# Peer routing stage: expert rows fetched a batch ahead, u's high part multiplied first, GELU stores on ScalarE's queue, and the second u tile's low part on VectorE

## The reference, cut to what matters

```
q = (xt @ w_q).reshape(T, PEER_HEADS, 2, PEER_HALF)
s = jnp.einsum('thpc,hpnc->thpn', q, sub_keys)
s_top, i_top = lax.top_k(s, PEER_TOPK)                     # 16 of 128 keys, twice per head
cand_s, cand_i = ...                                       # all 16 x 16 pairs
best_s, pos = lax.top_k(cand_s, PEER_TOPK)                 # 16 of 256 pairs, 8 heads
idx, gate = ..., jax.nn.softmax(best_s)                    # 128 experts of 16384 for each token
act = jax.nn.gelu(jnp.einsum('tkd,td->tk', u_tab[ib], xb), approximate=False)
out = jnp.einsum('tk,tkd->td', act * gb, v_tab[ib])
```

## Time and profile before

| what | value |
|---|---|
| median of 3 runs | 1585.91 us (1579.07 to 1590.8) |
| profiled execution | 1588.34 us, span 1586.6 us |
| PE busy | 1471.9 us (93%) |
| DVE busy | 1274.1 us (80%) |
| ACT busy | 824.7 us (52%) |
| POOL busy | 506.2 us (32%) |
| mean granted PE clock | 0.976 of 2.4 GHz |

### The profile page before, as it was taken

The page is one execution under the profiler, slowest core; times in us unless marked ns, Lnnn a source line. Parts: engine busy times, 40 slices in busy tenths (PEclk is TensorE's granted clock), DMA queues, the critical chain, the costliest instruction groups (busy, mean ns, idle before and its releaser), DMA issues.

```text
span 1586.6 us, 25321 instructions
## 1 busy us (share of the span) xinstructions
PE 1471.9 (93%) x9438; PEld 1325.3 (84%) x9438; DVE 1274.1 (80%) x2444; ACT 824.7 (52%) x1571; POOL 506.2 (32%) x425
## 2 busy tenths in 40 slices
PE   7999799999989888888897888999989999999999
PEld 6898688789889888888897887889878888888887
DVE  4638787776798697877867876999989999999997
ACT  4553453151434656655665854554455556565553
POOL 4011620110466666656661111322322222222220
PEclk9999899999999999989999999999999999999999
DMA  6220004030465788887889998999899999999993
GB/s 201 81 81 1 8 29 162 28 125 35 143 209 181 270 289 285 282 269 259 286 285 394 369 353 307 379 379 372 328 414 410 410 410 409 407 411 405 409 401 124
DMA packets 168439, 420.49 MB, mean 265 GB/s; under 512 B 12896, under 2 KB 100096, under 8 KB 151680
## 3 DMA queue, kind: packets, MB, share of 16 engines
q1 hardware_dynamic: 140608, 251.10, 44.8%
q0 software_dynamic: 27712, 167.82, 27.1%
HBM read 372.44 MB, written 46.40 MB: 264 GB/s over the span
## 4 chain that ended last, share of the span: by engine, by line
PE 55%; DMA 7%; DVE 4%; issue 4%; POOL 3%; ACT 2%; SPq 1%; ACTq 0%; DVEq 0%
PE bank L2432 7%; PE bank L2434 7%; PE bank L2433 7%; PE bank L2108 5%; PE bank L2109 5%; PE bank L2110 5%; DMA early_gelus<-early_gelu 5%; PE bank L2127 4%; PE banks L2432 3%; PE banks L2434 3%; PE banks L2433 3%; POOL u_split L2008 2%; PE bank L2420 2%; PE bank L2421 2%; PE bank L2422 2%
## 5 line engine op out<-in xcount | busy, mean ns | idle before, releaser
L2108 PE MATMUL bank<-x_hi,u_split 128*128 128x320 f32 x832 | 268.7, 323 | 7.8 <-POOL u_split L2008 7.3
L2109 PE MATMUL bank<-x_lo,u_split 128*128 128x320 f32 x832 | 260.3, 313 | 0.0
L2110 PE MATMUL bank<-x_hi,u_split 128*128 128x320 f32 x832 | 259.8, 312 | 0.0
L1804 POOL DMA_INDIRECT scores<-in_peer_uv,pair_index x86 | 106.7, 1241 | 392.2 <-DVE pair_sum L1828 391.2
L2108 PEld LDWEIGHTS bank<-x_hi,u_split 128*128 128x128 f32 x832 | 160.7, 193 | 12.2 <-issue 9.8
L2479 ACT ACTIVATE act_tile<-onehots 128x384 f32<-128x384 f32 x128 | 124.3, 971 | 82.3 <-DVE act_lo L2521 76.9
L2127 PE MATMUL bank<-onehot_j,onehot_gated 128*128 128x128 f32 x768 | 109.2, 293 | 58.6 <-issue 42.0
L2109 PEld LDWEIGHTS bank<-x_lo,u_split 128*128 128x128 f32 x832 | 160.4, 193 | 0.0
L2110 PEld LDWEIGHTS bank<-x_hi,u_split 128*128 128x128 f32 x832 | 159.8, 192 | 0.0
L2127 PEld LDWEIGHTS bank<-onehot_j,onehot_gated 128*128 128x128 f32 x768 | 100.9, 204 | 65.8 <-issue 65.1
L2008 POOL TENSOR_TENSOR u_split<-u_raw,u_split 128x1024 fp32r<-128x1024 f32 x41 | 99.2, 2420 | 119.8 <-ACT u_split L2165 61.2
(11 more groups left out here) (433 smaller groups left out, 4037.0 us busy)
## 6 DMA issues: line engine op xcount, KB each, us to landing
v_raw<-in_peer_v SPq DMA_DIRECT2D x128, 512.0 KB, 10.7
u_raw<-in_peer_u SPq DMA_DIRECT2D x64, 512.0 KB, 5.5
u_raw_more<-in_peer_u SPq DMA_DIRECT2D x64, 512.0 KB, 4.9
gates<-gate_stage SPq DMA_DIRECT2D x24, 1024.0 KB, 11.6
onehots<-gates SPq DMA_DIRECT2D x32, 768.0 KB, 11.6
early_gelus<-early_gelu SPq DMA_DIRECT2D x104, 160.0 KB, 4.8
gelu_tile<-early_gelus SPq DMA_DIRECT2D x104, 160.0 KB, 11.3
w_raw<-in_w_in SPq DMA_DIRECT2D x9, 1024.0 KB, 5.0
```

The costliest lines, as they stand in the source:

```text
L1804: pool.indirect_dma_start(self.slot(k), None, self.table, bass.IndirectOffsetOnAxis(ap=self.sidx[:, k:k + 1], axis=0)).then_inc(self.lande ...
L2108: nc.tensor.matmul(out, uh[:, q, w], m.xh[:, k, P + NS:], start=(k == 0), stop=False)
L2109: nc.tensor.matmul(out, uh[:, q, w], m.xl[:, k, P + NS:], start=False, stop=False)
L2110: t = nc.tensor.matmul(out, ul[:, q, w], m.xh[:, k, P + NS:], start=False, stop=(k == KD - 1))
```

## The change

Four edits, all in `routing`:

1. POOL fetches the rows one batch ahead: four fetches ahead of batch 0, then in each batch the two of the next batch, and they now stand ahead of the batch's low part.
2. POOL makes only the low part of a batch's first u tile. The second one's (24 tiles) goes to DVE, which makes the low parts of batch n+1 in its round n, right after `oj` of batch n and ahead of the selection part and the dots.
3. PE multiplies the 16 high-part matmuls of a u tile after a wait for `u_hi` alone, then waits for the low part, then multiplies the 8 low-part ones.
4. The GELU store goes from SP's list to ACT's, right behind the GELU. SP's list keeps the loads and the stores of gates.

```
-    pool_lows = list(range(1, FIRST)) + [t for n in range(LATE) for t in ups_of[n]]
+    pool_lows = list(range(1, FIRST)) + [t for n in range(LATE) for t in ups_of[n][:1]]
...
-                def tile(n):
-                    if n + 6 < EARLY + NU:
-                        load_u(n + 6)
-                    store_gelu(n)
-
...
                 for n in range(NB_):
                     for t in ups_of[n]:
-                        tile(t)
+                        load_u(t + NU)
                     if n % 2:
                         store_gates(n)
...
                 for n in range(LATE):
-                    for t in ups_of[n]:
-                        pool_low(t)
-                    for k in range(fetched, min(NS, fetched + DOTS)):
+                    for k in range(fetched, min(NS, fetched + (DOTS if n else 2 * DOTS))):
                         up_rows.fetch(pool, k)
                         fetched += 1
+                    for t in ups_of[n][:1]:
+                        pool_low(t)
...
                     banks.wait_free(pe, g)
-                    wait_low(pe, n)
+                    pe.wait_ge(u_hi, n + 1)
                     q, out = n % 2, banks.bank(g)[:, 0:TU]
                     for k in range(KD):
                         w = slice(k * P, (k + 1) * P)
                         nc.tensor.matmul(out, uh[:, q, w], m.xh[:, k, P + NS:], start=(k == 0), stop=False)
                         nc.tensor.matmul(out, uh[:, q, w], m.xl[:, k, P + NS:], start=False, stop=False)
+                    wait_low(pe, n)
+                    for k in range(KD):
+                        w = slice(k * P, (k + 1) * P)
                         t = nc.tensor.matmul(out, ul[:, q, w], m.xh[:, k, P + NS:], start=False, stop=(k == KD - 1))
...
                     nc.scalar.activation(ge[:, n % 2, 0:TU], banks.bank(("up", n))[:, 0:TU],
                                          ACT.Gelu).then_inc(banks.taken["act"], 1)
+                    banks.wait_taken(act, ("up", n))
+                    act.dma_start(gelus[n], ge[:, n % 2, 0:TU]).then_inc(nxt.ge_out[n % 2], 16)
...
-                    for t in range(ups_of[n][-1] + 1, EARLY - LAST if n + 1 == NB_ else ups_of[n + 1][-1] + 1):
+                    for t in range(ups_of[n][0] if n == 0 else ups_of[n][-1] + 1, EARLY - LAST if n + 1 == NB_ else ups_of[n + 1][-1] + 1):
                         if not low_count[t][0]:
                             early_low(t)
```

More of the change, by code:

```diff
@@ L2031, in load_u @@
                         sp.dma_start(u_raw[n % NU], u_t[n - EARLY]).then_inc(next_u[n % NU], 16)
-                def store_gelu(n):
-                    banks.wait_taken(sp, ("up", n))
-                    sp.dma_start(gelus[n], ge[:, n % 2, 0:TU]).then_inc(nxt.ge_out[n % 2], 16)
                 def store_gates(n):
@@ L2043, in store_gates @@
                                  stage[:, q].rearrange("p g t j -> p g (t j)")).then_inc(stored[q], 16)
-                def tile(n):
-                    if n + 6 < EARLY + NU:
-                        load_u(n + 6)
-                    store_gelu(n)
-                for n in range(2, 6):
+                for n in range(2, FIRST + NU):
                     load_u(n)
-                for n in range(FIRST):
-                    tile(n)
                 for n in range(NB_):
                     for t in ups_of[n]:
-                        tile(t)
+                        load_u(t + NU)
                     if n % 2:
@@ L2062, in _ @@
                             sp.dma_start(m.v_raw[i], v_rows[i]).then_inc(nxt.v_in[i], 16)
-                for n in range(EARLY - LAST, EARLY):
-                    tile(n)
+                for n in range(EARLY - LAST + NU, EARLY + NU):
+                    load_u(n)
                 for half in range(2):
```

## The result

The changed kernel takes **1743.49 us** (median of 3 runs, 1742.44 to 1745.02) where the kernel before took 1585.91. The ratio is 1.0992, with a 95% interval of 1.0937 to 1.1048: some 10% slower. The forecast was 1748 us in a range of 1685 to 1811.

What follows compares the result with a forecast made beforehand. The prediction took a ring of waits through PE, ACT's split, DVE and POOL to bound the batches. From the profiled 1588.3 us, +177 (batches), -7 (first part) and -8 (stores) gave 1750, as median 1748 us, range 1685 to 1811.

Steps and rivals of the forecast that it cites:

- The ring and its terms: In two-tile batches, PE, split, DVE's low part, selection, dots, fetches and POOL's low part wait in a circle: 17.3 us.
- The clock: After each PE stop of 8.5 us in the batches, the slow clock adds 2.5 us, making a turn 19.8 us.
- The batches: The part with the 32 batches goes from 310 to 487 us, +177 us, with bounds +156 and +198.
- E(0): The end on PE of batch 0's last u tile; 8 us plus some 3 us of the part lie ahead of it.
- 21 full turns: Steps between ends of successive batches on PE into two-tile batches, fetches and selection still running: 416 us together.
- High first: In the first part, 16 high-part matmuls cover PE's waits for POOL's low part: -7 us, between -3 and -8.
- The stores on ACT: In the last part, GELU stores issued from ACT take back 8 us; bounds -16 and +20.
- Rival 2: In the batches only DVE's half of the ring closes, POOL being early enough: total 1693 us; chance 0.06.
- Rival 3: In the batches DVE's slack takes the low parts without waiting: part 271 us, total 1532 us; chance 0.05.

Runs made afterwards that it cites:

- filler kernel: Changed kernel plus 70 matmuls into unread columns between a first tile's high-part matmuls and its wait for the low part, in 22 batches; 1721.61 us.
- the kernel with the fetches moved: Changed kernel with POOL's one low part of a batch issued ahead of the two row fetches; 1686.24 us.
- both reorderings: Changed kernel with DVE's low part behind the selection part and the dots, and POOL's fetches behind its low part; 1566.27 us.
- the fastest: Changed kernel with both low parts of a batch made by POOL again, the three other edits kept; 1531.15 us.

## Why the prediction was right

It was right in sign, size and mechanism; the fit of the single turn is in part luck, and one of the small terms is wrong. Its steps in turn:

- **The ring and its terms.** Over the 14 turns inside a group of batches the mean from low part to low part of DVE is 19.7 us (16.5 to 22.0), forecast 19.8. Split and low part 2.3 (forecast 2.4), selection 3.3 (3.2), dots 2.3 (2.3), from their end to PE's low-part matmuls 3.75 (3.8), PE's part with the clock 8.04 (5.6 + 2.5). The selection part varies from 0 to 5.2 us, and that is the spread of the turns. That edit 2 alone closes it is shown by the kernel without it.
- **The clock.** 0.79 in the part, inside the forecast 0.7 to 0.8. In the turn shown the clock was 0.56 in the window in which PE resumed, after a stop of 7.56 us. The term of 2.5 us a turn was 0.5 too large and PE's part without it 0.4 too small: at the full clock that part took 6.0 us in the filler kernel where the sum had 5.6, so that 2.0 of the 8.04 are the clock's. The two errors cancel, which is luck. The rule of the Trainium skill that was named (TensorE: Matmul & The Clock Gate, HAM oscillation) agrees with the trace here in that the loss comes again with the turns: in the turn shown the clock is 0.56 in 572:578 and back at 1.00 in 578:581. On the mean of each slice, the row of the 40 slices shows 0.7 and 0.8 through the whole part and 0.9 on both sides.

```profile
PEclk9999999999997787787778999999999999999999
```

- **The batches.** From E(0) to E(31), in the words of the prediction, 473.3 us passed, forecast 474 (35 + 416 + 23). The 21 full turns average 19.65 us, the last two are 11.7 and 13.3 (forecast 11.5), the eight steps into a one-tile batch 4.4 to 4.7. The +169.1 us between the evictions are less than the forecast +177 for what lies ahead: E(0) was forecast at 516 + 11 - 7 = 520 us and came at 516.2.
- **High first.** Forecast -7 in the first part. The single edit gave 6.8 there, and the changed kernel 9.6 with the stores and rows ahead as well. In all nine kernels with the edit the first eviction comes at 513.5 to 520.0 us, in the five without it at 523.3 to 528.7, so this term is shown.
- **The stores on ACT.** Forecast -8 in the last part. The changed kernel did gain 7.0 from the 64th eviction to `experts`, but **the step is wrong**: the single edit gained nothing there (127.5 against 127.0), and edits 1 and 3 without it reached 121.7. All kernels with edits 1 and 3 together take 120.0 to 122.7 us there (the filler kernel apart), those that lack one of the two 124.2 to 127.5. The 39.8 us that ACT waited for stores turned, in that single edit, into 22.4 us of waits for loads, at a DMA busy share that was already 1.03. Here the rule of the Trainium skill that the prediction named (DMA: Bandwidth & Descriptors, Issuing engines are not separate DMA queues), by which this term is near nothing, was the better forecast for that part (its total is 1748 + 8 = 1756, not the 1758 in the prediction). By which path edits 1 and 3 give the 5 to 7 us is open.
- **Rival 2**, only DVE's half closed, 1693 us: not the changed kernel, but the kernel with the fetches moved, at 1686. Its price was right, its condition did not hold.
- **Rival 3**, slack wins, 1532 us: no version with the low part on DVE comes near. The prediction ruled it out for the order in the ring. Its price for DVE's load, 271 us, was right (264.8 to 269.8 measured between the evictions); what fails is that DVE never waits. With both reorderings it still waited 25.7 us for splits in 515:800. The 1531 us belong to the three other edits.

In total, 1743.5 against 1748.

## What to carry to other kernels

Before work is moved to an engine that waits, write down what the moved instruction waits for and what is queued behind it on that engine. If a chain leads from that queue back to what it waits for, the idle time is no slack but part of a ring, and the ring's length, added up step by step, is the new period. Then look one round further: mending the order in one list left a longer path through the other, and mending that one left an engine without slack, on which every wait for a split still counted in full.

When edits are tried one by one, the verdict on an edit holds only for the limit of that moment. The store edit alone lost 0.8% and gained 1.2% behind the edit that removed the first limit, so it pays to try it again after each change of limit.

## What was not expected of the hardware

A stop of 2.64 us of PE, right behind the filler's 7.95 us of matmuls, was followed by low-part matmuls that took 2.33 us for eight in place of 1.17, in the filler run. Behind a stop of 1.74 us they took 2.47 us (at 764.66), behind another of 1.75 us only 1.45 (at 587.96), each right behind the same burst. So the length of the stop alone did not decide. The prediction's stops were 8.5 us, and it had no row for such short ones.

VectorE's and GpSimd's low parts (both read two SBUF tiles) hardly run side by side: in the kernel with DVE's low part behind the dots, a DVE low part that met one of POOL's ended 1.08 or 1.09 us after it in all six cases that were longer than 1.3 us, and took up to 4.12 us in place of 1.23. The changed kernel has such a case at the end of the first part (3.74 us at 507.65). So where a low part falls in time matters, and not only its length.

A GELU store of 160 KB moved from SP's queue to ACT's costs ACT a wait of up to 0.7 us ahead of the eviction behind it, 16.5 us in 38 pieces in 515:800 of the kernel with that edit alone. That kernel was slower, and DVE's waits for fetched rows grew there by 10.5 us. Whether they grew by ACT's later one-hots and splits or by another order of the transfers is not settled; in the kernels with the rows ahead the same pieces stand (21.5 us in the fastest), and the edit gains.
